# A two-layer token mixer on eight cores: another order of work in the first tiles and of the transfers at the passage between the layers

## The reference

```python
def fourier_mixer(h, w_in, w_out):               # layer 0
    proj = h @ w_in                              # (4096, 1024) @ (1024, 4096)
    xin, z = proj[..., :2048], proj[..., 2048:]
    xg = xin.reshape(b, s, 8, 256)
    y = jnp.fft.fft2(xg, axes=(1, 3), norm="ortho").real
    return (y.reshape(b, s, 2048) * jax.nn.silu(z)) @ w_out

def sgu_mixer(h, w_in, v_ln_g, v_ln_b, w_s, b_s, w_out):   # layer 1
    proj = h @ w_in                              # (4096, 1024) @ (1024, 6144)
    u, v = split(gelu(proj[..., :4096])); z = proj[..., 4096:]
    v = layer_norm(v) reshaped to (chunks of 128 positions, 8 groups of 256)
    v = einsum('gpq,bnqgc->bnpgc', w_s, v) + b_s
    return (u * v * jax.nn.silu(z)) @ w_out
```

## Time and profile before

| | us |
|---|---|
| median of 3 runs | 1580.16 |
| lowest of them | 1579.46 |
| profiled execution | 1582.04 |
| its span (core 1, the slowest) | 1580.7 |
| TensorE busy in it | 1545.7 (98%) |
| VectorE, ScalarE, GpSimd busy | 747.1, 515.9, 156.4 |

### The profile page before, as it was taken

One profiled execution on the slowest core, in us unless ns is written; L12 is line 12 of the kernel. 1 busy time (PEld: TensorE's weight loads), 2 busy tenths in 40 slices (PEclk: granted clock), 3 DMA queues, 4 the chain that ended last, 5 costly groups with the idle time before them and its releaser, 6 DMA issues.

```text
span 1580.7 us, 25439 instructions; the slowest of 8 cores (1564.3 to 1580.7 us)
## 1 busy us (share of the span) xinstructions
PE 1545.7 (98%) x8458; PEld 782.7 (50%) x8458; DVE 747.1 (47%) x1245; ACT 515.9 (33%) x915; POOL 156.4 (10%) x336
## 2 busy tenths in 40 slices
PE   6999999999899999999999999999999999999997
PEld 3557766646644444544444444445444444544443
DVE  5866532213636435624553463356245435624552
ACT  5766333333223313322331232133123313322331
POOL 3311111010211011001000100110010011001000
PEclk9999999999999999999999999999999999999999
DMA  9986999999887941643453155335324531643411
GB/s 256 288 249 170 171 139 152 152 144 180 250 205 189 242 176 48 226 150 98 152 199 125 38 188 199 107 116 201 134 69 167 207 113 47 226 152 96 148 46 54
DMA packets 103298, 247.72 MB, mean 157 GB/s; under 512 B 40042, under 2 KB 56042, under 8 KB 87402
## 3 DMA queue, kind: packets, MB, share of 16 engines
q1 hardware_dynamic: 53652, 207.76, 39.8%
q0 software_dynamic: 15568, 29.63, 14.9%
q10 hardware_dynamic: 33952, 8.72, 3.3%
HBM read 225.24 MB, written 58.87 MB: 180 GB/s over the span
## 4 chain that ended last, share of the span: by engine, by line
PE 94%; DMA 4%; DVE 1%; issue 1%; ACT 0%; SPq 0%; POOL 0%; DVEq 0%; ACTq 0%; POOLq 0%
PE pf L848 28%; PE pf L751 27%; PE pf L412 14%; PE pf L821 14%; PE pf L595 5%; PE pf L858 2%; DMA gy<-sz_77 1%; DMA a0x_59<-xt 1%; DMA gyt<-gy 1%; PE pb L481 1%; PE pf L491 1%; PE pf L558 1%; DMA h1T<-xn_0_2525 1%; PE pf L431 1%; SPq L166 0%
## 5 line engine op out<-in xcount | busy, mean ns | idle before, releaser
L751 PE MATMUL pf<-W_2513,gyt 128*128 128x512 bf16 x992 | 219.2, 382 | 7.4 <-DMA gyt<-gy 7.4
L751 PE MATMUL pf<-W_2524,u 128*128 128x512 bf16 x1024 | 222.3, 379 | 0.0
L751 PEld LDWEIGHTS pf<-W_2513,gyt 128*128 128x128 bf16 x992 | 97.6, 98 | 126.6 <-issue 13.0
L751 PEld LDWEIGHTS pf<-W_2524,u 128*128 128x128 bf16 x1024 | 100.2, 98 | 120.8
L851 ACT ACTIVATE u<-pf 128x512 bf16<-128x512 f32 x128 | 76.5, 597 | 164.2 <-PE pf L848 154.7
L825 ACT ACTIVATE v<-pf 128x512 f32<-128x512 f32 x128 | 75.4, 597 | 121.1 <-PE pf L821 101.6
L848 PE MATMUL pf<-h1T,ring_2522 128*128 128x512 bf16 x416 | 96.8, 385 | 0.0
L848 PE MATMUL pf<-h1T,ring_2519 128*128 128x512 bf16 x416 | 96.5, 382 | 0.0
L848 PE MATMUL pf<-h1T,ring_2523 128*128 128x512 bf16 x416 | 95.5, 380 | 0.0
L848 PE MATMUL pf<-h1T,ring_2520 128*128 128x512 bf16 x416 | 94.9, 379 | 0.0
L848 PE MATMUL pf<-h1T,ring_2521 128*128 128x512 bf16 x384 | 88.3, 379 | 0.0
(11 more groups left out here) (298 smaller groups left out, 2317.8 us busy)
## 6 DMA issues: line engine op xcount, KB each, us to landing
ring_2519<-wind SPq DMA_DIRECT2D x20, 1024.0 KB, 7.4
ring_2520<-wind SPq DMA_DIRECT2D x19, 1024.0 KB, 7.1
ring_2521<-wind SPq DMA_DIRECT2D x19, 1024.0 KB, 6.7
ring_2522<-wind SPq DMA_DIRECT2D x19, 1024.0 KB, 7.1
ring_2523<-wind SPq DMA_DIRECT2D x19, 1024.0 KB, 6.4
gyt<-gy SPq DMA_DIRECT2D x7, 2048.0 KB, 12.4
wind<-w_in1p POOLq DMA_DIRECT2D x24, 512.0 KB, 42.1
V<-ud SPq DMA_DIRECT2D x32, 256.0 KB, 7.9
```

The source lines that it names most:

```text
L751: pe.op(lambda e: e.matmul(bank[:], lhs(kc), rhs[:, kc, nh * 512:(nh + 1) * 512], start=(kc == 0), stop=(kc == 15)), lb(kc) + rb(kc), [bb] ...
```

## The change

In the head: `norm(1)` and `norm(2)` go from ahead of the loop into it. Two tables (`first`, `then`) say after which step a norm stands and whether ahead of or behind the evacuation into hT. The transform with its evacuations runs one tile behind (`due`), up to tile 23; for tiles 0 to 3 ScalarE evacuates both halves. The first zgroup stands ahead of tile 4's transposes. Weight tile 1 is loaded in step 0, 2 in step 1, and so on up to 4, and 5 in step 6.

In the passage: x1(0), x1(1), x1(2) and g1t are loaded after gyt, behind a wait of SP for both halves of gyt to land. Ring buffers are numbered one on, so that rings 0 to 3 are loaded between the parts of group 7 and ring 4 into buffer 0 after gate(7), behind x1(3). From group 6 on `tick()` leaves four stores in the list (`keep`): those of kc = 12 to 15. Each of them is issued after one of the first four `send1`, behind a wait of SP for that transpose to land; the last store of g67 follows the fourth.

```diff
@@ the head
             square(1)
-            norm(1)
-            load_wz(1)
             square(2)
-            norm(2)
             zq = []
             behind = []
+            due = []
+            first = {1: [2], 2: [3], 4: [5]}
+            then = {0: [1], 1: [], 2: [], 3: [4], 4: [6], **{s: [s + 2] for s in range(5, 10)}, 10: [12, 13]}
+
+            def transform(r):
+
+                xn_, xnb = xn[r % 4]
+                U_, Ub = U[r % 8]
+                for h in range(2):
+                    bank, bb = next_f()
+                    pe.op(lambda e: e.matmul(bank[:], tr[:], xn_[:, h * 512:(h + 1) * 512],
+                                             start=True, stop=True),
+                          [trb, xnb], [bb], waw=False)
+                    copy_on((act, dve)[h if r > 3 else 0], U_[:, h * 512:(h + 1) * 512], bank[:], [bb], [Ub])
+                behind.append(r)
+
@@ in the loop
+                if s == 4:
+                    zgroup(*zq.pop(0))
                 xn_, xnb = xn[s % 4]
-                U_, Ub = U[s % 8]
...
+                for n in first.get(s, []):
+                    norm(n)
                 dve.op(lambda e: e.tensor_tensor(
                     out=hT[:, :, s * 128:(s + 1) * 128],
...
-                for h in range(2):
...
-                    copy_on((act, dve)[h], U_[:, h * 512:(h + 1) * 512], bank[:], [bb], [Ub])
-                for _ in range(1 + (s % 4 == 3 and s < 16)):
+                due.append(s)
+                while len(due) > (s < 24):
+                    transform(due.pop(0))
+                for _ in range((s != 4) + (s % 4 == 3 and s < 16)):
                     if zq:
                         zgroup(*zq.pop(0))
                 if s + 3 < 32:
                     square(s + 3)
-                behind.append(s)
...
-                if s + 3 < 32:
-                    norm(s + 3)
-                if s in (0, 1, 2, 5):
-                    load_wz(2 + s if s < 3 else 5)
+                for n in then.get(s, [s + 3] if 10 < s < 29 else []):
+                    norm(n)
+                if s in (0, 1, 2, 3, 6):
+                    load_wz(1 + s if s < 4 else 5)
@@ tick
-                if stores and ticks["n"] % 4 == 0:
+                if len(stores) > keep["n"] and ticks["n"] % 4 == 0:
                     stores.pop(0)()
@@ pq
                     if g == 7 and 0 < qd < NR:
-                        load_ring(qd)
+                        load_ring(qd - 1)
@@ load_ring, and alike in vtile and wide
-                    k = n % NR
+                    k = (n + 1) % NR
@@ send1
                 act.dma_t(h1T[:, :, t * 128:(t + 1) * 128], j_[:], d_t[t], [jb], [h1Tb[t]])
+                if n < 4:
+                    sp.wait((d_t[t].sem, d_t[t].n))
+                    stores.pop(0)()
+                    if n == 3:
+                        sp.dma(gsp[6:8], g67[:, :], d_67, reads=[g67b], writes=gyTb[13:16:2], waw=True)
@@ the loop over groups
                 if g == 7:
-                    load_ring(0)
                     load_x1(3)
-                if g == 7:
-                    while stores:
-                        stores.pop(0)()
+                    load_ring(4)
@@ at g == 4
-                    for n in range(3):
-                        load_x1(n)
-                    sp.dma(g1t[:], g1.partition_broadcast(128), d_g1, writes=[g1b], waw=True)
@@ at g == 6
+                    keep["n"] = 4
...
                     sp.dma(gyt[:, 1:12:2, :], even[1, :, 0:6, 0:512], d_g, reads=gyTb[1:12:2], writes=[gytb], more=True)
+                    sp.wait((d_g.sem, d_g.n))
+                    for n in range(3):
+                        load_x1(n)
+                    sp.dma(g1t[:], g1.partition_broadcast(128), d_g1, writes=[g1b], waw=True)
@@ after the loop over groups
-            sp.dma(gsp[6:8], g67[:, :], d_67, reads=[g67b], writes=gyTb[13:16:2], waw=True)
```

More of the change, by code:

```diff
@@ L526, in build @@
             stores = []
+            keep = {"n": 0}
             late = []
@@ L817, in vtile @@
                 for j in range(4):
-                    r_, rb = ring[(12 * i + j) % NR]
+                    r_, rb = ring[(12 * i + j + 1) % NR]
                     bank, bb = next_f()
@@ L843, in wide @@
                 n = 12 * i + 4 + 4 * k + ct // 4
-                r_, rb = ring[n % NR]
+                r_, rb = ring[(n + 1) % NR]
                 c0 = (ct % 4) * 128
```

## The result

The kernel after takes 1566.82 us (median, 1564.49 to 1570.53) against 1580.81 us of the kernel before beside it: a ratio of 0.992, 95% interval 0.989 to 0.994. The forecast was 1568.1 us. On the chip of the first four experiments cores 4 to 7 ran at a lower clock whatever the kernel, which hides their times, so those four are compared by cores 0 to 3, in the executions that show these at a granted clock of 0.99 or more.

What follows compares the result with a forecast made beforehand. PE was taken as the bound, each core's losses before its first vtile deciding its span. Core 3's 448.1 + 1123.1 = 1571.2, less 2.5 for the head, plus 1.3, minus 1.9 gave 1568.1 us (own range 1564 to 1572).

Steps and rivals of the forecast that it cites:

- The last step, from that span to the median: End of the sum: add 1.3 us for execution over span, take off 1.9 for the profiled execution standing above the median.
- The bound, that a core's losses before its first vtile decide its span: Whole kernel: PE is nearly always busy, so what a core loses before its first vtile sets its span.
- signs of being wrong: PE waiting for a0xn between 26 and 50, gyt after 421, ring wait near 484, or tails above 1125 us.
- Head, to transposes 8: First tiles: transposes 8 start at 33.0 instead of 36.56, less 1.0 for weights; gain 2.5 us, bounds 0.7 and 3.5.
- the 1.0 us for earlier weight loads: Head: weight loads 2 to 4, about 3 us earlier, delay tile 6 by 0 to 1.9 us; 1.0 taken.
- After transposes 8 PE has no gap, so the gain is kept to the passage: Between head and passage: no PE gap after transposes 8, so the head's 2.5 us reach the passage whole.
- head without gain: Rival, head: tiles 4 to 8 arrive so much later that PE waits for them; 1570.6 us, chance 0.14.
- Passage, chain of the stores: Layer 0 to 1: sz_77 lands near 406.4, gy<-szsp goes at 407.6, gyt lands at 417.6, before PE needs it.
- That it would keep its 12.5: Rival, passage: gyt's odd half still takes 12.5 us, stalling PE 1.0 plus 2 at lower clock; 1571.1 us, chance 0.12.
- Passage, the transposed load: First h1T transpose goes near 441.0, vtile starts at 449.4: 8.4 us of cover, no PE wait taken.
- the slower rival: Passage, SP's queue: held stores take 28.5 us each, ring 5 comes at 503.0, PE stalls 18.7; 1586.8 us, chance 0.03.
- Tails: From first vtile to the end: 1119.9 us on core 1 and 1123.1 on core 3, kept from the kernel before.

Runs made afterwards that it cites:

- first four experiments: Kernel before with head alone (slowest of cores 0 to 3: 1576.7 us), passage alone (1563.5), x loads alone moved (1579.6, 1579.0); kernel after without SP's gyt wait (1564.6 to 1568.6).
- experiments 1 and 2: Kernel before with only the head's edits, then only the passage's: slowest of cores 0 to 3 ended at 1576.7 and 1563.5 us, against 1577.9 before.
- experiment 10: Kernel after with weight loads 2 to 4 one step later; transposes 8 at 33.3 to 34.2 us against 31.6 to 32.2; no total time given.
- experiments 6 to 8: Kernel after with step 24's second transform behind the zgroup (1564.1 us); norms two ahead to the end (1560.55 us); transform lag removed (transposes 31 at 97.0 to 97.6).
- experiment 3: Kernel after without SP's wait for gyt to land; slowest of cores 0 to 3 ended at 1564.6 to 1568.6 us.
- experiment 5: Kernel after with layer 0's last stores not held for the transposes; the profiled execution took 1577.7 us.
- run 11: Kernel after repeated unchanged on another chip: 1564.00 us, ratio 0.9935 to the kernel before.
- run 12: Kernel after with norms two ahead to the end and norm(1) ahead of hT(0): 1561.12 us, ratio 0.9914 to the kernel before.

## Why the prediction was right, and where it was not

The total was right to 1.3 us, but by luck: terms of the sum were off and cancelled. By the sum core 3 was the slowest. Its first vtile came 1.2 us later than said (446.82 against 445.6), and its tail was 7.0 us shorter (1116.1 against 1123.1), so that the slowest span was 1563.1 and not 1568.7. The last step, from that span to the median, was put at -0.6 us and came to 3.7: the profiled execution was the quickest of the four, and in each of the others one core or several ended later (core 2 at 1569.1 in the slowest). What keeps those cores back stays open. The bound, that a core's losses before its first vtile decide its span, holds in the kernel after, where all tails are 1116.0; in the kernel before the tails differed by core as well. Of the signs of being wrong one showed, but small: on seven cores PE waited 0.3 to 1.1 us for a0xn between 26 and 50, with transposes 8 at 32.4 to 33.3.

- **Head, to transposes 8.** Said 2.5 us; core 1 gained 3.9, cores 0 to 3 of one chip 3.2 on the mean (experiments 1 and 2). The term that was mis-sized is the 1.0 us for earlier weight loads: later weights brought tile 6 no earlier (experiment 10), and cost 2.0 us on the mean at transposes 8. Tile 6 came at 20.99 on core 1, not later than 22.76 as said; in the kernel before, core 1's 22.76 was the latest of the four cores (20.42 to 22.76), so one core's row carried that bound.
- **"After transposes 8 PE has no gap, so the gain is kept to the passage": the step that failed.** It was read from the kernel before, which has norms, squares and banks in another order. In the kernel after PE waits 1.8 us for U_70 and 1.1, 0.6 and 1.3 us for hT on cores 0, 1 and 3 past transposes 8, the later transform takes 0.43, and transposes 31 come about where they came before (core 3: 100.36 and 100.40; core 1: 101.34 and 99.62). The sentence that the later transform needs its banks no longer than before is true, 5.0 us before and after, and is where the prediction should have stopped: not the time a bank is held, but the fifth bank of a step and VectorE's order set the wait. The rival "head without gain" had the right outcome by the wrong cause: not the inputs, but VectorE behind ScalarE's square (experiments 6 to 8).
- **Passage, chain of the stores: right.** The chain ran as said, 3 us earlier throughout since POOL's gate started at 395.57 instead of 398.74: gy<-szsp at 404.53 (said 407.6, bounded by that gate), no wait for gyt or h1T on core 1, out0 27.63 us (said 27.6), first vtile on core 1 at 445.86 (said 446.9 with the head), on core 3 at 446.82 (said 445.6). The odd half took 5.3 us, not 7.5. That it would keep its 12.5 was given 0.12; experiment 3 shows 12.2 without the wait.
- **Passage, the transposed load: right for too weak a reason.** I took no wait and allowed 2.3 us with the old 10.7; seven cores had none and core 5 had 0.7. Without the held stores it is 16 to 20 us on cores 0 to 3 and a stall of 8 to 11 (experiment 5). The held stores, which I treated as a risk for SP, carry the gain; they landed in 4.0 to 5.1 us, ring 5 went at 468.55 (said 468), and the slower rival never came near.
- **Tails.** Said 1119.9 and 1123.1, as measured on cores 1 and 3 of the kernel before; measured 1116.0 and 1116.1. In the kernel before, cores 0 and 1 share the tail of 1119.9 and cores 2 and 3 that of 1123.1, while cores 4 to 7 have 1116.0. The extra is stretches of 4 to 8 us in the middle of uninterrupted matmuls with a granted clock of 0.81, at the same moments on both cores of a pair: four after the first vtile on cores 0 and 1, eight on cores 2 and 3. One of them, core 1 (columns as in the earlier trace rows, with POOL last of the engines):

```profile
810.80:816.00 5.20, 5.20 (x24) 2.32 (x23) 2.84 (x6) 1.29 (x3) 0.00 (x0) 0.81 1.06 367
```

In the profile of the kernel after no core has any. The kernel with the head alone had tails of 1116.0 on cores 0 to 3 with waits for gyt up to 11.5 us, so the waits before the first vtile don't cause it; what does stays open. That the change removes these stretches is not shown: on the chip of the first four experiments they come on cores 4 to 7 with each of the four kernels, and on cores 0 to 3 with none. Of the 17.6 us between the slowest cores of the two profiled executions (1580.7 and 1563.1), 3.8 are such a tail, and about 3 more three such stretches on core 1 ahead of its first vtile (an estimate from their 17.2 us at 0.81). The smaller gain on another chip, some 10 us in run 11 (0.9935), is in line with that.

## What to carry to other kernels

A lead won at the start of a pipeline is worth only what the loop behind it passes on: follow it through the changed loop's own order, engine by engine, and ask of each in-order engine which operand of the current step it stands at. Small transfers that gate the next stage should have the queue to themselves: hold bulk stores behind them, and measure the next transfer too, since clearing one only exposes its neighbour. Where a sum comes out right, look at its terms on several cores before trusting it.

## What the runs showed of the hardware

A wait of PE costs more than its length. In experiment 5, core 2, after the wait for h1T (windows; the number behind POOL's count is the granted clock):

```profile
456.00:460.00 4.00, 3.66 (x9) 1.31 (x10) 2.57 (x3) 1.09 (x2) 0.00 (x0) 0.50 0.66 172
```

The granted clock is 0.50, the lower level of 1.2 GHz, through these 4 us after the wait, and that experiment's tails are 2.4 to 2.8 us longer on cores 0 to 3.

The same gaps don't cost the same on every core. In the version of run 12, cores 6 and 7 show equal waits on PE ahead of the zgroup at 143 us (0.47, 0.39 and 0.20 against 0.47, 0.38 and 0.19), but core 6:

```profile
143.76 3.35 PE L412 MATMUL pf<-hT,wz 128*128 128x512 bf16 x8
```

and core 7:

```profile
142.74 1.89 PE L412 MATMUL pf<-hT,wz 128*128 128x512 bf16 x8
```

The granted clock between 142 and 146 is 0.66 on the mean on core 6 and 1.00 on core 7, which costs core 6 1.7 us until pq(0), all of its distance to the other cores (444.3 against 442.8 and less). What tells the two cores apart stays open.
